# Second attention of a two-block transformer kernel: lower parts of the weights, first scores and pooling products in another order

## What is computed

```
proj = h @ w_in                                  # 1024 x 2304
q, k, v, ga, u, gb = split(proj)                 # 512, 128, 128, 512, 512, 512
ya = sliding_window_attention(q, k, v, sinks) * silu(ga)   # 8 heads of 64, 2 key heads, blocks of 128,
                                                           # each block sees itself and the one before
yb = multiscale_pool(u, pool_w, pool_scale) * silu(gb)     # 4 groups of 128 channels, windows 2, 4, 8, 16
y = concatenate([ya, yb]) @ w_out                # 1024 x 1024
x = x + rms_norm(y)
# multiscale_pool: pooled = mean of the window - u; y = pooled_g @ pool_w_g for each group, times pool_scale
```

## Time and profile before

| | |
|---|---|
| median of 3 executions | 1041.22 us (1037.6 to 1041.86) |
| the profiled execution | 1038.82 us |
| its span, first to last instruction | 1037.0 us |
| mean granted clock of TensorE | 0.992 of full speed |
| TensorE matmuls busy | 997.4 us, 96% of the span |
| VectorE, ScalarE, GpSimd busy | 565.3, 397.3, 58.4 us |

### The profile page before, as it was taken

One profiled execution on the slowest core, in us unless ns is written; L12 is line 12 of the kernel. 1 busy time (PEld: TensorE's weight loads), 2 busy tenths in 40 slices (PEclk: granted clock), 3 DMA queues, 4 the chain that ended last, 5 costly groups with the idle time before them and its releaser, 6 DMA issues.

```text
span 1037.0 us, 12886 instructions
## 1 busy us (share of the span) xinstructions
PE 997.4 (96%) x5280; PEld 804.2 (78%) x5280; DVE 565.3 (55%) x765; ACT 397.3 (38%) x646; POOL 58.4 (6%) x49
## 2 busy tenths in 40 slices
PE   4999999999999999999999999989889999999997
PEld 3977787878888888888888878768768886677786
DVE  2346766657441343344334483365554766889963
ACT  4235663376333341134133354243463721222551
POOL 2100102000000000000000000013000100000300
PEclk9999999999999999999999999989999999999999
DMA  6832102233222323322224214302041465655121
GB/s 194 154 98 79 41 2 82 96 121 118 100 95 82 121 82 113 131 82 82 82 90 146 90 41 135 126 35 82 1 148 44 128 186 143 171 145 166 50 82 81
DMA packets 63362, 104.84 MB, mean 101 GB/s; under 512 B 3974, under 2 KB 27399, under 8 KB 63176
## 3 DMA queue, kind: packets, MB, share of 16 engines
q1 hardware_dynamic: 62968, 103.77, 31.7%
q10 hardware_dynamic: 336, 0.25, 0.1%
HBM read 99.43 MB, written 4.58 MB: 100 GB/s over the span
## 4 chain that ended last, share of the span: by engine, by line
PE 84%; DVE 9%; ACT 3%; issue 3%; DMA 1%; ACTq 0%; DVEq 0%
PE acc L791 24%; PE acc L792 24%; PE acc L793 24%; PE ps L1076 2%; PE psT L1061 1%; PE psT L950 1%; PE acc L1050 1%; PE psT L929 1%; DVE wlr L1819 1%; DVE psT L2201 1%; DMA hot<-in_onehot_dram 1%; ACT wh L1446 1%; PE ps L950 1%; ACT lg L1528 1%; DVE sm L1937 1%
## 5 line engine op out<-in xcount | busy, mean ns | idle before, releaser
L1819 DVE TENSOR_TENSOR wlr<-wl,wh 128x2048 fp32r<-128x2048 f32 (+1 forms) x66 | 145.2, 2204 | 77.7 <-ACT wh L1446 77.7
L791 PE MATMUL acc<-act_hi,wh 128*128 128x512 f32 x464 | 184.8, 398 | 0.3 <-DVE wlr L1819 0.3
L793 PE MATMUL acc<-act_hi,wlr 128*128 128x512 f32 x464 | 181.7, 392 | 0.0
L792 PE MATMUL acc<-act_lo,wh 128*128 128x512 f32 x464 | 181.6, 391 | 0.0
L1446 ACT ACTIVATE wh<-wl 128x2048 fp32r<-128x2048 f32 (+1 forms) x68 | 124.3, 1832 | 58.7 <-DMA wl<-in_w_up_dram 35.7
L791 PE MATMUL acc<-wh,act_hi 128*128 128x512 f32 (+1 forms) x352 | 133.6, 380 | 0.0
L793 PE MATMUL acc<-wh,act_lo 128*128 128x512 f32 (+1 forms) x352 | 130.6, 371 | 0.0
L792 PE MATMUL acc<-wlr,act_hi 128*128 128x512 f32 (+1 forms) x352 | 130.4, 370 | 0.0
L791 PEld LDWEIGHTS acc<-act_hi,wh 128*128 128x128 f32 x464 | 87.9, 189 | 23.1 <-issue 4.2
L793 PEld LDWEIGHTS acc<-act_hi,wlr 128*128 128x128 f32 x464 | 87.6, 189 | 18.7
L792 PEld LDWEIGHTS acc<-act_lo,wh 128*128 128x128 f32 x464 | 87.8, 189 | 17.3
(11 more groups left out here) (237 smaller groups left out, 1422.6 us busy)
## 6 DMA issues: line engine op xcount, KB each, us to landing
wl<-in_w_up_dram SPq DMA_DIRECT2D x16, 1024.0 KB, 6.5
wl<-in_w_down_dram SPq DMA_DIRECT2D x16, 1024.0 KB, 7.3
wl<-in_c_w_in_dram SPq DMA_DIRECT2D x20, 512.0 KB, 4.9
raw<-in_w_in_dram SPq DMA_DIRECT2D x18, 512.0 KB, 4.8
shifted<-glu_dram SPq DMA_DIRECT2D x32, 262.0 KB, 4.7
wl<-in_a_w_in_dram SPq DMA_DIRECT2D x8, 1024.0 KB, 6.2
wl<-in_w_out_dram SPq DMA_DIRECT2D x4, 1024.0 KB, 6.3
wl<-in_ab_w_out_dram SPq DMA_DIRECT2D x4, 1024.0 KB, 7.4
```

What stands on the lines that cost most here:

```text
L791: pe.matmul(dst, hi, x_hi, start=first, stop=False)
L792: pe.matmul(dst, hi, x_lo, start=False, stop=False)
L793: return pe.matmul(dst, lo, x_hi, start=False, stop=last)
L1819: dve.tensor_tensor(wlr[slot][:, kk, cols], wl[slot][:, kk, cols], wh[slot][:, kk, cols].bitcast(F32), ALU.subtract).then_inc(wlo_done, 1)
```

## The change

Four things are done. The step `wsplit` of N_GB and N_AO0 becomes two steps: `upper` (ScalarE's part alone) in units 2, 4, 10 and 12, `lower` (VectorE's part alone) in units 3, 5, 11 and 13. Before, both were in units 2, 3, 10 and 11. Query tile 3 becomes the work of unit 0, and scores 0 wait for query tile 1 only; so the other 16 half tiles come one unit later, in units 1 to 16. The sums of the pooling go to other units (`pool_window` in 2, 4, 6, 8, `pooled` in 4, 7, 9, 12). The last turn is no longer in unit 17: after unit 16 come pooling products 2 and 3, turn 3, pooling products 0 and 1, then the other engines' share as the step `branches`, in the order of channels 6, 7, 4, 5. The out-projection reads its channels in the same order.

```
--- before.py
+++ after.py
@@ -560,19 +560,24 @@
         def mixer2_steps():
             steps = [("wtile", N_KV, 0), ("wsplit", N_Q, 0), ("wtile", N_KV, 1), ("wsplit", N_Q, 1),
                      ("wtile", N_Q, 0), ("keys_values", 1), ("wtile", N_Q, 1), ("wsplit", N_U, 0),
-                     ("wtile", N_Q, 2), ("wsplit", N_U, 1), ("wtile", N_Q, 3)]
-            halves_left = [("wtile", n, m, h) for n in (N_U, N_GB) for m in range(4) for h in range(2)]
-            splits = {2: (N_GB, 0), 3: (N_GB, 1), 10: (N_AO0, 0), 11: (N_AO0, 1)}
-            for k in range(STEPS + 2):
-                work = [halves_left[k]] if k < len(halves_left) else []
-                if k in splits:
-                    work.insert(0, ("wsplit",) + splits[k])
-                if k in (1, 3, 5, 7):
-                    work.append(("pool_window", k // 2))
-                if k in (3, 5, 8, 11):
-                    work.insert(0, ("pooled", (3, 5, 8, 11).index(k)))
+                     ("wtile", N_Q, 2), ("wsplit", N_U, 1)]
+            halves_left = [("wtile", N_Q, 3)]
+            halves_left += [("wtile", n, m, h) for n in (N_U, N_GB) for m in range(4) for h in range(2)]
+            uppers = {2: (N_GB, 0), 4: (N_GB, 1), 10: (N_AO0, 0), 12: (N_AO0, 1)}
+            lowers = {3: (N_GB, 0), 5: (N_GB, 1), 11: (N_AO0, 0), 13: (N_AO0, 1)}
+            pooled = (4, 7, 9, 12)
+            for k in range(STEPS + 1):
+                work = [halves_left[k]]
+                if k in uppers:
+                    work.insert(0, ("upper",) + uppers[k])
+                if k in lowers:
+                    work.insert(0, ("lower",) + lowers[k])
+                if k in (2, 4, 6, 8):
+                    work.append(("pool_window", k // 2 - 1))
+                if k in pooled:
+                    work.insert(0, ("pooled", pooled.index(k)))
                 steps += attention_unit(k, work)
-            return steps + [("pool_out", 0)]
+            return steps + [("pool_out", 2), ("pool_out", 3), ("turn", 3), ("pool_out", 0), ("pool_out", 1), ("branches", 0)]
 
         def window(layer, n):
 
@@ -1041,7 +1046,7 @@
                     if i == 0:
                         pe.wait_ge(kx_done, 2 * (layer + 1))
                     if i < 4 and layer == 1:
-                        pe.wait_ge(evD_done, evacs_before(TILE_AT[N_Q, 3 if i == 0 else i], "D") + 1)
+                        pe.wait_ge(evD_done, evacs_before(TILE_AT[N_Q, max(i, 1)], "D") + 1)
                     if k >= 1:
                         pe.wait_ge(logits_done, k)
                     for j in range(2):
@@ -1163,13 +1168,17 @@
                 elif what == "gla_sum":
                     gla_sum(i)
                 elif what == "pool_out":
-                    pe.wait_ge(mix2_in, 16 * MIX2_LOADS)
-                    pe.wait_ge(o_done, 8)
-                    pe.wait_ge(vtok_done, 2)
-                    for g in range(4):
-                        pe.wait_ge(pooled_done, g + 1)
-                        dst = (ps6[:, :], ps7[:, :], psT[:, 0, :], psT[:, 1, :])[g]
-                        pe.matmul(dst, pw[:, g, :], uu[:, g, UPAD:], start=True, stop=True).then_inc(yb_ps, 1)
+                    if i == 2:
+                        pe.wait_ge(mix2_in, 16 * MIX2_LOADS)
+                        pe.wait_ge(pooled_done, 4)
+                        pe.wait_ge(pTs_done, 2 * STEPS)
+                    elif i == 0:
+                        pe.wait_ge(oq_done, 2 * STEPS)
+                    elif i == 1:
+                        pe.wait_ge(o_done, 8)
+                        pe.wait_ge(vtok_done, 2)
+                    dst = (ps6[:, :], ps7[:, :], psT[:, 0, :], psT[:, 1, :])[i]
+                    pe.matmul(dst, pw[:, i, :], uu[:, i, UPAD:], start=True, stop=True).then_inc(yb_ps, 1)
 
             for at, step in enumerate(STEPS_OF[0]):
                 mixer_step_pe(0, step, at)
@@ -1238,11 +1247,11 @@
                         weights(N_AO0, half)
                     if half == 0:
                         bank_free(TILE_AT[N_AO0, b])
-                    for k in range(4 * half, 4 * half + 4):
+                    for m, k in enumerate((0, 1, 2, 3, 6, 7, 4, 5)[4 * half:4 * half + 4], 4 * half):
                         if b == 0:
-                            pe.wait_ge(act_lo_done, 8 * 2 + k + 1)
+                            pe.wait_ge(act_lo_done, 8 * 2 + m + 1)
                         last = mm3(acc[:, b, :], act_hi[:, k, b * P:(b + 1) * P], act_lo[:, k, b * P:(b + 1) * P],
-                                   wh[N_AO0 % 2][:, k, :], wlr[N_AO0 % 2][:, k, :], k == 0, k == KT - 1)
+                                   wh[N_AO0 % 2][:, k, :], wlr[N_AO0 % 2][:, k, :], m == 0, m == KT - 1)
                     if half == 1:
                         last.then_inc(wtile_done, 1)
             out_boundary(2, N_AO1)
@@ -1508,7 +1517,7 @@
                 k = 16 * layer + i
                 if what in ("split", "split_hi"):
                     split(i)
-                elif what == "wsplit":
+                elif what in ("wsplit", "upper"):
                     hi(i, step[2])
                 elif what == "keys_values":
                     if layer == 0:
@@ -1574,14 +1583,14 @@
                     halves(o1, (4, 5), lambda e, k: e.wait_ge(o_done, 4))
                     hi(N_O0, 0)
                     halves(o1, (6, 7), lambda e, k: e.wait_ge(o_done, 4))
-                elif what == "pool_out":
+                elif what == "branches":
                     act.wait_ge(wtile_done, CHUNK_END[N_GB])
                     halves(o2, (0, 1, 2, 3), lambda e, k: e.wait_ge(o_done, 8))
-                    for h in range(4):
+                    for h in (2, 3, 0, 1):
                         act.wait_ge(evD_done, evacs_before(TILE_AT[N_GB, h], "D") + 1)
                         act.activation(gb2[:, h, :], gb2[:, h, :], ACT.Silu).then_inc(silu2_done, 1)
                     exp_ln_tables()
-                    halves(o2, (4, 5, 6, 7), lambda e, k: e.wait_ge(ob_done, k - 3))
+                    halves(o2, (6, 7, 4, 5), lambda e, k: e.wait_ge(ob_done, (3, 4, 1, 2)[k - 4]))
 
             def head_scale(h):
 
@@ -1899,7 +1908,7 @@
                 k = 16 * layer + i
                 if what in ("split", "split_lo"):
                     split(i)
-                elif what == "wsplit":
+                elif what in ("wsplit", "lower"):
                     lo(i, step[2])
                 elif what == "wtile":
                     if step[3:] != (0,):
@@ -2036,17 +2045,17 @@
                     dve.scalar_tensor_tensor(out=uu[:, i, UPAD:], in0=wsum[:, i % 2, UPAD:], scalar=1.0 / POOLW[i],
                                              in1=uu[:, i, UPAD:], op0=ALU.mult, op1=ALU.subtract)\
                        .then_inc(pooled_done, 1)
-                elif what == "pool_out":
+                elif what == "branches":
                     lower_halves(o2, (0, 1, 2, 3), 2, 0)
-                    for g in range(4):
-                        dve.wait_ge(silu2_done, 1 + g)
-                        dve.wait_ge(yb_ps, g + 1)
+                    for m, g in enumerate((2, 3, 0, 1)):
+                        dve.wait_ge(silu2_done, 1 + m)
+                        dve.wait_ge(yb_ps, m + 1)
                         src = (ps6[:, :], ps7[:, :], psT[:, 0, :], psT[:, 1, :])[g]
                         dve.scalar_tensor_tensor(out=o2[:, 4 + g, :], in0=src, scalar=vec[:, V_PSC + g:V_PSC + g + 1],
                                                  in1=gb2[:, g, :], op0=ALU.mult, op1=ALU.mult).then_inc(ob_done, 1)
-                        if g >= 1:
-                            lower_halves(o2, (3 + g,), 2, 3 + g)
-                    lower_halves(o2, (7,), 2, 7)
+                        if m >= 1:
+                            lower_halves(o2, ((6, 7, 4, 5)[m - 1],), 2, 3 + m)
+                    lower_halves(o2, (5,), 2, 7)
 
             def gla_normed(h):
                 dve.wait_ge(rr_done, h + 1)
```

## The result

| | before | after |
|---|---|---|
| median | 1040.15 us (4 runs, 1037.6 to 1041.86) | 1023.68 us (4 runs, 1023.03 to 1025.3) |
| ratio after / before | | 0.9842, 95% interval 0.9824 to 0.9861 |
| profiled execution, its span | 1038.82, 1037.0 | 1025.3, 1023.5 |
| mean granted clock | 0.992 | 1.0 |
| TensorE busy | 997.4 us | 993.3 us |

The kernel is 16.5 us faster by the medians and 16.0 by the means; 17.4 were forecast, and the interval of the ratio allows 14.5 to 18.3. The time forecast was 1022.5 us, 1.2 under the median measured.

A forecast was written before the change was run, and what follows sets the result against it. TensorE sets the pace, with 18.3 us lost to idle time and lower clock (0.8 + 12.8 + 4.7). Less 0.3, 0.2 and 0.35, some 17.4 us are gained: from a mean of 1039.9 to 1022.5 us, range 1018.5 to 1028.5.

The forecast's parts named there:

- Query tile: At the first scores: the 0.8 us wait for query tile 3's evacuation goes, and nothing takes its place.
- Middle: Five attention windows: 12.8 us over full speed, 8.1 of it idle time, would go, less 0.3 for turn 0.
- ideal of 5.05: Middle window of 9.00 us: full-speed length, from 5.44 less some 0.4 for its one-block products.
- I leave 0.3 us in all for turn 0: Middle, turn 0: 0.3 us allowed because its gating stands behind `pooled` 0 and a later softmax.
- the copy of 1.02 us in the earlier trace: Small VectorE copy beside GpSimd's pooling windows: 1.8 us of cover, so cost of 0 to 3.4 us taken as 0.
- End: Last two windows, 11.02 us against 6.33 of full-speed work: 4.7 us gained, less 0.35 of new out-projection wait.
- The 0.2 left for transfers: Weight transfers of GB and AO0 before their first upper parts: tight, 0.2 us allowed for both together.
- Clock: TensorE's granted clock stays at its upper level once idle time goes; 5.8 us of the gain is clock.
- The rival in which the clock swings on and 5.8 us stay: TensorE's clock swings though idle time is gone: 5.8 us of the gain lost, 1028.3 us; chance 0.06.
- two units in a row: Units 10 and 11: weight steps form one serial loop, upper parts 7.26 us apart against 4.80 for an undisturbed unit.
- Load against length: Middle units: each engine's load must fit the unit; ScalarE 4.24 and VectorE 4.20 us, both under 4.80.

The follow-up runs named there:

- e4: Changed kernel with GpSimd's pooling window 1 made to wait until gating 0 is done; ratio to the kernel before 0.9844, median 1023.88 us.
- e1: Kernel before with only the lower parts moved a unit later (upper in 2, 4, 10, 12, lower in 3, 5, 11, 13); ratio to before 0.9878.
- e6: Changed kernel with upper parts in units 2, 3, 10, 11 and lower parts a unit later, in 3, 4, 11, 12; ratio to before 0.9856.
- e8: Changed kernel with upper and lower part in the same unit, in 2, 6, 10 and 14, spaced and away from gating; ratio to before 0.9932.
- e9: Changed kernel with upper and lower part in the same unit, in rows 5, 6 and 13, 14, away from gating; ratio to before 0.9961.
- e5: Changed kernel with upper and lower part in the same unit, spaced, in 2, 4, 10 and 12; ratio to before 0.9941.
- e3: Changed kernel with turn 3 put ahead of all four pooling products again; ratio to the kernel before 0.9862.
- e2: Changed kernel with upper and lower part back in the same unit, in 2, 3, 10 and 11; ratio to the kernel before 0.9932.

## Why the prediction was right

- **Query tile, 0.8 forecast.** The wait of scores 0 is gone and no other took its place.
- **Middle, 12.8 less 0.3 forecast.** Gained 11.9: of the five windows only that of 5.90 is clearly above its ideal of 5.05, by 0.85. The step mis-sized is "I leave 0.3 us in all for turn 0": it waited 0.87. e4 takes GpSimd's sum from beside the gating, and 0.30 is left. I had counted such stretches, from the copy of 1.02 us in the earlier trace rows, as covered. I looked for them at small copies only and not at the gating, on which a turn waits.
- **End, 4.7 less 0.35 forecast.** The two windows of before, 11.02, compare with 4.22 + 5.28 less the half tile of 2.74, that is 6.76: 4.26 gained, with a wait of 0.42 at the out-projection. The slower start of the first matmul behind that wait takes 0.23 more, which the forecast didn't have.
- **Sum.** 0.8 + 11.9 + 4.3 = 17.0 of the stretch's 17.10. The 0.2 left for transfers were not needed: ScalarE began upper part 0 at 679.62, right behind its exponentials.
- **Clock.** 1.00 all through, as taken; TensorE's busy time in the stretch fell from 97.29 to 90.46 us, for the same matmuls. The rival in which the clock swings on and 5.8 us stay did not come. Its source, the Trainium skill (TensorE: Matmul & The Clock Gate, "A second HAM failure mode: psum-queue depth-cycling"), speaks of a clock that swings on micro-idles. The kernel before fits that: its clock of 0.62 from 692.75 us on came with gaps of 0.60, 0.71, 2.05, 0.64 and 0.83 us. The changed kernel, which cycles through the same banks, has one gap of 0.87 in the middle and 1.00, so the cycling alone does not bring the swing.
- **The reason given for the middle was half right.** The 12.8 us were read off the windows, so the sum needed only that the change removes the delay, whatever makes it. I put the lag down to "two units in a row" and wrote that the loop is cut when the parts are in different units. The cut is shown by e1 and e6. But the row is the smaller share: a weight step in one unit costs 2.1 us alone (e8) and a row 2.3 more for each pair (e9, with the reserve on its units), and by the one trace of e5 a step ahead of a gating costs about as much again. The forecast of the change didn't hang on it, the forecast of e5 did, and missed by 8 us.
- **Load against length was too strict a test.** e1 has a unit with 5.6 us of VectorE work and lost 0.15 us.

What stays open: the share of the clock. Idle time of 1.18 and 0.78 us in e3 didn't bring it down, and 0.54 and 0.92 in e8 did; I have not settled what tells them apart.

## What to carry to other kernels

Where one engine's step needs another engine's step, put them in different units of an in-order list: then neither sits idle at the head of its queue with the pacing engine's work behind it. Here that was worth 10.1 us for four steps (e2). Spacing such pairs out doesn't replace this (e5, e8). Before placing a long step, look at what is queued behind it and which of that is needed first (here the gating, on which the turn waits), and use a product that waits for nothing to cover the last hop of a chain.

## What the hardware showed

In these traces the gating and the lower part, VectorE instructions with both operands in SBUF, and a GpSimd sum don't run side by side: the one that comes second waits for about the rest of the first. The gating started 0.35 us into GpSimd's 1.06 us, with 0.71 left, and took 1.26 instead of 0.69; GpSimd's sum started 0.26 us into the lower part's 2.28, with 2.02 left, and took 2.94 instead of 1.06. The Trainium skill says so (SBUF — State Buffer, "Who interferes with whom": the pair of ports that VectorE and GpSimd share is an exclusive lock, and issue order decides who blocks), and the trace agrees in both directions. The small copies beside GpSimd's sums are held too (1.02 us at 691.17, 0.16 elsewhere); the softmax instruction that reads `acc` in PSUM is not (0.68 at 716.75, in the midst of three sums). I had not expected it at the gating. It makes the place of a GpSimd step a matter of which VectorE instruction it falls on, even where GpSimd itself is never waited for.
